# Expert weights in a ring of sixteen slots, one transfer per matrix

## The chip, the core and the metric

The kernel runs on one core of one Trainium2 chip. The time is device microseconds (us) of one execution. Beside it stands one execution taken by the hardware profiler, whose instructions and DMA packets the rows below come from. Engine names: PE is TensorE, DVE VectorE, ACT ScalarE, POOL GpSimd, SP SyncE. Everything is in 32-bit floats.

## The reference

One batch of 256 tokens, width 1024, goes through a first block (adaptive norm, gated linear attention, block attention, a dense feed-forward network) and a second one (dilated attention, a convolution, then a mixture of experts). Two thirds of the time is the last line of this:

```python
aff = softmax(h @ w_router)                      # 256 x 16
gate, idx = lax.top_k(aff.swapaxes(1, 2), 32)    # each of 16 experts takes 32 tokens
def expert(xt, w1e, w3e, w2e):                   # w1, w3: 1024 x 2816; w2: 2816 x 1024
    return (silu(xt @ w1e) * (xt @ w3e)) @ w2e
x = x + scatter_add(expert(h[idx_e], ...) * gate_e   for e in range(16))
```

Each expert has three matrices of 11.5 MB, read once: 34.6 MB an expert, 554 MB in all, for only 32 tokens each.

## The kernel before

The first 600 us hold everything up to the router. SP streams the dense matrices in "units" of three slots through an SBUF tile `ring`; PE works on them with intermediate results in a second tile, `arena`.

Then the expert phase. A slot is 2816 words a partition, 11 KB, and one matrix is 8 slots, so that an expert is 24 chunks, q = 0 to 23: w1 is 0 to 7, w3 is 8 to 15, w2 is 16 to 23. `ring` has 12 slots, and chunk q of every expert lies in slot q mod 12 (24 is a multiple of 12). SP is the only one that issues weight transfers, all on one queue (L363 to L407). It cuts an expert into eight pieces, `PIECES = (4, 4, 4, 4, 4, 2, 1, 1)` chunks (L40), each with its own semaphore `piece_in[i]`. Before each it waits on `w_used`, which PE raises by one with the last matmul of each chunk: the piece may start when the chunks that lay in its slots have been used.

PE's program for an expert is `expert(e)` (L1749). `gather` picks the 32 tokens by 16 matmuls of 32 columns with a one-hot matrix; ACT copies them to `xe` (L734). Then come the 64 matmuls of w1 (four tiles of 32 columns side by side, 352 wide), two transposes (L1791), and the 64 of w3. ACT and DVE form silu(a)*b and transpose it (L738, L1197, L1201, L1205) to `hTe`; the 88 matmuls of w2 follow; ACT copies the result out (L743); 8 matmuls scatter it with the gate weights, and DVE adds it to the output rows (L1208). Waits on `piece_in` stand at the first chunk of each piece. Expert 0 is written out, experts 1 to 15 are a loop of 15 turns (L1824).

Expert 0 is special, since its weights come while the earlier part still runs. Chunks 0 to 11 go to the ring early. Chunks 12 to 15, the last four of w3, go to `stash`, four slots' worth at the start of `arena` (L249), which are free by then. So the ring's slots 0 to 3 can take the first four chunks of expert 1 (in pieces of 1, 1 and 2, at `w_used` 1, 2 and 4) before w2 of expert 0 starts at `w_used` 8. After expert 0 the stash is not used again. `pick`, `aff` and the other live tiles of the phase lie in `arena` behind it.

A 32-bit matmul is four PE instructions (two weight loads, two passes), so the traces count two MATMUL for each one in the program. The compiled PE program has 7,843 instructions, and the body of its loop 994.

Of the kernel before, what the change touches and what calls it, by code (L numbers as in the profile page):

```python
# [15 lines left out]
C = D // P  # L16
# [16 lines left out]
FR = FE // P  # L33
DG = D // 4

SLOT = FE
NSLOT = 12
BLOCK = 3 * SLOT
NCHUNK = 24
PIECES = (4, 4, 4, 4, 4, 2, 1, 1)  # L40
AR = 14536


# [13 lines left out]
                  ("conv_ln_g_2", 4), ("conv_ln_b_2", 4), ("q_norm_g_2", 1), ("k_norm_g_2", 1)):  # L57
    VEC[_name] = (sum(n for _, n in VEC.values()), _n)
NVEC = sum(n for _, n in VEC.values())

PIECE_AT = [(sum(PIECES[:i]), n) for i, n in enumerate(PIECES)]
PIECE_OF = {q: i for i, (q, n) in enumerate(PIECE_AT)}
assert sum(PIECES) == NCHUNK and all(q % C + n <= C and q % NSLOT + n <= NSLOT for q, n in PIECE_AT)


def bank_plan():
# [53 lines left out]
def build(nc, T, out, rel_dram):  # L120
    PLAN = bank_plan()
    with ExitStack() as ctx:
        def sb(name, cols):
            return ctx.enter_context(nc.sbuf_tensor(name, [P, cols], F32))

        def sem(name):
            return ctx.enter_context(nc.semaphore(name))

        ring = sb("ring", NSLOT * SLOT)
        arena = sb("arena", AR)  # L130
        xT_ = sb("xT", C * S)
        hT_ = sb("hT", C * S)
        ident = sb("ident", P)
# [21 lines left out]
        def ex(off, words, **dims):  # L155
# [90 lines left out]
        csq = ar(0, 1024, m=CT)  # L246
        halfgb = small[:, 88:96]

        stash = ar(0, 4 * SLOT)  # L249
        yacc = xT_[:, :].rearrange("p (st n) -> p st n", st=ST)  # L250
        hnat = hT_[:, :].rearrange("p (st n) -> p st n", st=ST)
        pick = ar(11264, 1024, st=ST)
# [17 lines left out]
        emptied = [sem(f"bank_emptied{b}") for b in range(8)]  # L270
        unit_in = [sem(f"unit_in{b}") for b in range(3)]
        unit_in2 = sem("unit_in_gate_columns")
        piece_in = [sem(f"piece_in{i}") for i in range(len(PIECES))]
        s = {name: sem(name) for name in """
            x_in table_in ident_in rest_in mv_in shift_set gbias_set grs_set xg_set pv_set unit_used w_used const_set e_set attz_set attd_set
            att_set hid_used consts2_in upz_set conv_set cm_set acc_set gg2_set u2_set den_set epsd_set r1_set xr_set rsq_set qc_set cmean_set crec_set
# [1 line left out]
            sq0_set n0_set rtbneg_set relW_in t0_set hT_set ggT_set gqk_set z_set zl_set gv_set  # L278
            gr_set sgr_set b_set mqk_set klnat_set mv_set o_set osq_set gla_n max_set exp_set pT_set xmid_set
            sq1_set n1_set t1_set h_set relu_set x1_set sq2_set n3_set n2_set up_set sgb_set pe_link  # L280
            qsq_set qk_set rs16_set v_set    csq_set diag_set cvar_set x2_set sq3_set first_in stash_in lead_in sqp_set
            lge_set wr2_set std_set rst_set lgs_set hnat_set yinit_set xe_set ye_set xe_full sc_full pgT_set hid_full he_set sg_set
            ye_full out_done dve_link adacol_set adarow_set amix_set gla_set S_set mixg_set p_set
            mixm_set h2_set rs16i_set qn_set rt_set qf_set mixa_set aff_set rank_set
# [41 lines left out]
        @block.sync  # L326
        def _(sp):
            def rows(ap, c0, n):
                return ap[:, c0:c0 + n].rearrange("(c p) n -> p c n", p=P)

            def unit_source(name):
                if name.startswith("ada"):
                    return rows(T["w_ada"], D * int(name[3]), D)
                if name.startswith("win_"):
                    c0, n = {"a": (0, 2 * QKW), "v": (512, 512), "r": (1024, 512), "c": (1552, 1024)}[name[4]]
                    return rows(T["w_in"], c0, n)
                if name == "wout":
                    return rows(T["w_out"], 0, D)
                if name.startswith("ff1"):
                    return rows(T["w_ff1"], D * int(name[4]), D)  # L340
                if name.startswith("ff2"):
                    u = int(name[4])
                    return rows(T["w_ff2"][u * D:(u + 1) * D, :], 0, D)
                if name in ("conv", "qk", "v"):
                    c0, n = {"conv": (3 * MW, 2 * CW), "qk": (0, 2 * MW), "v": (2 * MW, MW)}[name]
                    return rows(T["w_in_2"], c0, n)
                return rows(T["w_out_2"], 0, D)


            for i, name in enumerate(UNITS):  # L350
                if i >= 3:
                    sp.wait_ge(s["unit_used"], FREED.index(UNITS[i - 3]) + 1)
                src = unit_source(name)
                n = src.shape[2]
                unit = unit_ap(name, C, 1024 if name == "win_v" else n)
                sp.dma_start(unit[:, :, 0:n], src).then_inc(unit_in[i % 3], 16)
                if name == "win_a":
                    o = (1 + i % 3) * BLOCK + C * 512
                    sp.dma_start(ring[:, o:o + C * RANK].rearrange("p (c n) -> p c n", c=C),
                                 rows(T["w_in"], 1536, RANK)).then_inc(unit_in2, 16)  # L360
                if name == "win_v":
                    sp.dma_start(unit[:, :, n:], rows(T["w_in"], 2576, 512)).then_inc(s["mv_in"], 16)

            mats = [T["w1_2"].rearrange("e (p c) f -> p e (c f)", p=P), T["w3_2"].rearrange("e (p c) f -> p e (c f)", p=P),
                    T["w2_2"].rearrange("e (p r) n -> p e (r n)", r=FR)]

            def slots(e, q, n, done):
                at, mat = q % NSLOT, q // C
                sp.dma_start(ring[:, at * SLOT:(at + n) * SLOT],  # L369
                             mats[mat][:, e, (q - C * mat) * SLOT:(q - C * mat + n) * SLOT]).then_inc(done, 16)  # L370

            def piece(e, i):
                slots(e, *PIECE_AT[i], piece_in[i])

            sp.wait_ge(s["unit_used"], UNIT["qk"] + 1)
            slots(0, 9, 3, s["first_in"])
            sp.wait_ge(s["unit_used"], UNIT["v"] + 1)
            sp.wait_ge(s["qf_set"], 4)
            sp.wait_ge(s["conv_set"], TAPS * CT)
            sp.wait_ge(s["xr_set"], 1)  # L380
            piece(0, 0)
            slots(0, 4, 2, s["first_in"])
            sp.wait_ge(s["unit_used"], UNIT["wo2"] + 1)
            slots(0, 6, 2, piece_in[1])
            slots(0, 8, 1, piece_in[2])
            stashed = mats[1][:, 0, (12 - C) * SLOT:]
            sp.dma_start(stash[:, 0:3 * SLOT], stashed[:, 0:3 * SLOT]).then_inc(s["stash_in"], 16)
            sp.wait_ge(s["std_set"], 1)
            sp.dma_start(stash[:, 3 * SLOT:], stashed[:, 3 * SLOT:]).then_inc(piece_in[3], 16)
            for q, n, done in ((0, 1, s["lead_in"]), (1, 1, s["lead_in"]), (2, 2, piece_in[0])):  # L390
                sp.wait_ge(s["w_used"], q + n)
                slots(1, q, n, done)
            for i, (q, n) in enumerate(PIECE_AT):
                if q > 12:
                    sp.wait_ge(s["w_used"], q + n - NSLOT)
                    piece(0, i)
            for i, (q, n) in enumerate(PIECE_AT):
                if q > 0:
                    sp.wait_ge(s["w_used"], NCHUNK + q + n - NSLOT)
                    piece(1, i)  # L400
            with sp.Fori(0, NE - 2) as e:
                for i, (q, n) in enumerate(PIECE_AT):
                    sp.wait_ge(s["w_used"], NCHUNK * e + q + n + 2 * NCHUNK - NSLOT)
                    piece(e + 2, i)


        @block.gpsimd  # L407
# [806 lines left out]
        def _(pe):  # L1214
# [531 lines left out]

            pe.sem_inc(s["pgT_full"], 1)
            pe.sem_inc(s["sc_full"], 1)
            def expert(e, first=False):  # L1749
                def gather(g):  # L1750
                    for c in range(4 * g, 4 * g + 4):
                        for st in range(ST):
# [9 lines left out]
                for mat, bank in enumerate((0, 2)):  # L1762
                    for c in range(C):
                        q = mat * C + c
                        slot = q % NSLOT
                        if mat == 0:
                            pe.wait_ge(s["xe_set"], C * e + c + 2)
                        if q in PIECE_OF:
                            pe.wait_ge(piece_in[PIECE_OF[q]], 16 * (e + 1))
                        w = ring[:, slot * SLOT:(slot + 1) * SLOT]  # L1770
                        if first and q >= 12:
                            w = stash[:, (q - 12) * SLOT:(q - 11) * SLOT]
                            pe.wait_ge(s["stash_in"], 16)
                        elif first and q >= 4:
                            pe.wait_ge(s["first_in"], 32)
                        elif q == 0 and not first:
                            pe.wait_ge(s["lead_in"], 32)
                        for half in range(2):
                            for j in range(4):
                                c0 = j * FG + half * FH  # L1780
                                ins = mm(ps[32 * j:32 * j + CAP, bank + half, 0:FH], xe[:, c, :], w[:, c0:c0 + FH],
                                         c == 0, c == C - 1)
                        ins.then_inc(s["w_used"], 1)
# [8 lines left out]
                        ins.then_inc(s["pgT_full"], 1)  # L1792
                pe.wait_ge(s["hTe_set"], e + 1)
                pe.wait_ge(s["pgT_set"], e + 1)
                w2v = ring[:, 4 * SLOT:12 * SLOT].rearrange("p (r n) -> p r n", r=FR)
                got = 0
                for r in range(FR):
                    while got * SLOT < (r + 1) * D:
                        q = 2 * C + got
                        if q in PIECE_OF:  # L1800
                            pe.wait_ge(piece_in[PIECE_OF[q]], 16 * (e + 1))
                        got += 1
                    for j in range(4):
                        ins = mm(ps[32 * j:32 * j + CAP, 4, 0:DG], hTe[:, r, :], w2v[:, r, j * DG:(j + 1) * DG],
# [15 lines left out]
                                 ye[32 * j:32 * j + CAP, :], True, True)  # L1820
                    ins.then_inc(s["sc_full"], 1)

            expert(0, first=True)
            with pe.Fori(1, NE) as e:  # L1824
                expert(e)


def S_at(Sst, n, mt):
# [83 lines left out]
```

## Time and profile before

| | us |
|---|---|
| median of 3 runs | 1854.61 |
| lowest, highest | 1854.27, 1855.59 |
| the profiled execution's own time | 1853.62 |
| its span, first to last instruction | 1851.9 |

Around the span 1.72 us of the profiled execution are outside the instructions. It lies 0.99 us under the median. In the span, PE has records for 73% of the time, PE's weight loads for 45%, DVE 15%, ACT 12%, POOL 2%. 649 MB are moved.

### The profile page before, as it was taken

The page shows a single profiled execution, that of the slowest core. Times are in us where ns is not written, and L with a number is a line of the kernel's source. Part 1 is how long each engine was busy: PE and PEld are TensorE (multiplying, and loading weights), DVE is VectorE, ACT ScalarE, POOL GpSimd, SP SyncE. Part 2 cuts the span into 40 slices and gives each one's busy share as a digit, 9 for nine tenths or more (in the row PEclk, how much of TensorE's full clock was granted, in tenths as well). Part 3 has the DMA queues.
Part 4 walks back from the last instruction along what each step waited for, and adds up shares of the span by engine and source line. Part 5 has one row for each costly group of instructions (what it writes and reads, how often), then busy time and mean ns, then how long its engine had stood idle before and what let it go on. Part 6 is the DMA issues. An engine that isn't in the chain of part 4 may idle for free.

```text
span 1851.9 us, 24026 instructions
## 1 busy us (share of the span) xinstructions
PE 1353.7 (73%) x10574; PEld 831.9 (45%) x10574; DVE 274.7 (15%) x559; ACT 226.6 (12%) x530; POOL 39.4 (2%) x64
## 2 busy tenths in 40 slices
PE   6998999999987777476666757566655665756665
PEld 4576888888655334142332414234232322413232
DVE  1215100006952001000010100001000000100001
ACT  1333222012133010000100001010000100000010
POOL 0000000002020000000000000000000000000000
PEclk9999999999998777777777777877777787777778
DMA  9746363341444899999999999999999999999998
GB/s 351 299 163 242 114 250 145 128 182 68 185 187 187 372 436 435 427 430 433 438 428 429 435 429 435 430 435 435 427 431 428 442 422 436 435 431 426 430 441 342
DMA packets 48248, 649.02 MB, mean 350 GB/s; under 512 B 3832, under 2 KB 6336, under 8 KB 31056
## 3 DMA queue, kind: packets, MB, share of 16 engines
q1 hardware_dynamic: 45152, 643.90, 82.4%
q10 hardware_dynamic: 2848, 3.55, 0.6%
q0 software_dynamic: 208, 1.00, 0.1%
q8 instruction: 30, 0.49, 0.1%
q14 instruction: 10, 0.08, 0.0%
HBM read 647.38 MB, written 1.06 MB: 350 GB/s over the span
## 4 chain that ended last, share of the span: by engine, by line
DMA 59%; PE 11%; DVE 1%; ACT 1%; issue 0%; SPq 0%; PEldq 0%; DVEq 0%; ACTq 0%
DMA ring<-in_w 59%; PE ps L1216 11%; DVE arena L1113 0%; ACT arena L678 0%; ACT arena L525 0%; DVE arena L1164 0%; DVE arena L1166 0%; DVE xT L1208 0%; ACT L701 0%; ACT L678 0%; ACT arena L688 0%; ACT arena L687 0%; DVE arena L1183 0%; SPq L369 0%; DVE arena L1079 0%
## 5 line engine op out<-in xcount | busy, mean ns | idle before, releaser
L1216 PE MATMUL ps<-ring,table 128*32 128x352 f32 x4032 | 435.3, 602 | 269.4 <-DMA ring<-in_w 269.3
L1216 PEld LDWEIGHTS ps<-ring,table 128*32 128x32 f32 x4032 | 154.1, 140 | 535.5 <-issue 340.4
L1216 PE MATMUL ps<-ring,arena 128*32 128x256 f32 (+1 forms) x2818 | 197.3, 438 | 148.9 <-DMA ring<-in_w 148.6
L1216 PEld LDWEIGHTS ps<-ring,arena 128*32 128x32 f32 (+1 forms) x2818 | 103.2, 125 | 245.1 <-issue 149.0
L1216 PE MATMUL ps<-hT,ring 128*128 128x256 f32 (+1 forms) x880 | 194.6, 382 | 3.0 <-PE ps L1216 1.4
L1216 PEld LDWEIGHTS ps<-hT,ring 128*128 128x128 f32 (+1 forms) x880 | 165.0, 189 | 30.8 <-issue 5.9
L1216 PE MATMUL ps<-arena,ring 128*128 128x256 f32 (+1 forms) x800 | 175.1, 379 | 1.9 <-ACT arena L627 1.4
L1216 PEld LDWEIGHTS ps<-arena,ring 128*128 128x128 f32 x800 | 151.5, 190 | 23.3 <-issue 2.9
L1216 PE MATMUL ps<-arena 32*128 32x256 f32 (+10 forms) x532 | 96.4, 396 | 31.7 <-DVE xT L1208 12.2
L1216 PEld LDWEIGHTS ps<-arena,hT 128*128 128x128 f32 x512 | 106.3, 320 | 9.4 <-issue 9.4
L1216 PE MATMUL ps<-arena,hT 128*128 (+1 forms) x512 | 108.4, 392 | 1.8 <-DVEq L1192 1.8
L743 ACT ACTIVATE arena<-ps 128x256 f32<-128x256 f32 x16 | 6.2, 384 | 731.0 <-PEq L1809 731.0
L1208 DVE TENSOR_TENSOR xT<-xT,ps 128x512 f32<-128x512 f32 x64 | 41.8, 685 | 343.7 <-PE ps L1216 343.7
L1216 PEld LDWEIGHTS ps<-arena 32*128 32x128 f32 (+7 forms) x532 | 62.5, 189 | 64.6 <-issue 34.5
L1197 DVE TENSOR_TENSOR arena<-arena,ps 128x704 f32<-128x704 f32 x16 | 14.2, 888 | 429.7 <-ACT arena L738 429.7
L1201 DVE TENSOR_TENSOR arena<-arena,ps 128x704 f32<-128x704 f32 x16 | 14.2, 888 | 376.3 <-PEq L1785 376.3
L1014 DVE SCALAR_TENSOR_TENSOR arena<-arena,table 128x256 f32<-128x256 f32 x120 | 52.9, 508 | 1.2 <-DVE arena L1048 0.2
L738 ACT ACTIVATE arena<-ps 128x704 f32<-128x704 f32 x16 | 12.1, 758 | 285.6 <-PEq L1785 285.6
L1216 PE MATMUL ps<-ring,hT 128*128 128x512 f32 x96 | 44.5, 615 | 0.5 <-ACT hT L520 0.4
L734 ACT ACTIVATE table<-ps,table 128x32 f32<-128x32 f32 x128 | 26.3, 288 | 140.2 <-PE ps L1216 140.2
L1216 PE MATMUL ps<-ring 128*128 128x256 f32 (+5 forms) x200 | 41.0, 388 | 2.2 <-PE ps L1216 1.4
L466 POOL TENSOR_TENSOR arena<-arena 128x128 f32 x32 | 12.1, 399 | 1168.1 <-PE ps L1791 1105.2
(223 smaller groups left out, 542.8 us busy)
## 6 DMA issues: line engine op xcount, KB each, us to landing
ring<-in_w SPq DMA_DIRECT2D x76, 5632.0 KB, 32.9
ring<-in_w SPq DMA_DIRECT2D x19, 2816.0 KB, 28.4
ring<-in_w SPq DMA_DIRECT2D x35, 1408.0 KB, 31.3
ring<-in_w_ff SPq DMA_DIRECT2D x8, 4096.0 KB, 14.0
ring<-in_w_ada SPq DMA_DIRECT2D x6, 4096.0 KB, 13.8
ring<-in_w_in SPq DMA_DIRECT2D x3, 4096.0 KB, 14.4
ring<-in_w_in SPq DMA_DIRECT2D x5, 2048.0 KB, 19.2
ring<-in_w_out SPq DMA_DIRECT2D x2, 4096.0 KB, 12.8
```

The costliest lines, as they stand in the source:

```text
L466: ins = nc.gpsimd.tensor_tensor(pgs[:, st, :].rearrange("p (j t) -> p j t", j=4), pick[:, st, bass.ds(e * CAP, CAP)].unsqueeze(1).broadcas ...
L734: A(xe[:, c, :], ps[:, (7, 3)[c // 4], c * CAP:(c + 1) * CAP], ACT.Copy, scale=g2rows[:, c:c + 1])\
L738: A(sge.rearrange("p (a b) -> p a b", a=2), ps[:, 0:2, 0:FH], ACT.Sigmoid).then_inc(s["sg_set"], 1)
L743: A(ye, ps[:, 4, 0:DG], ACT.Copy).then_inc(s["ye_set"], 1)
L1014: ins = V.scalar_tensor_tensor(dst, src, w, dst, ALU.mult, ALU.add)
L1197: V.tensor_tensor(he.rearrange("p (a b) -> p a b", a=2), sge.rearrange("p (a b) -> p a b", a=2), ps[:, 0:2, 0:FH], ALU.mult).then_inc(s["h ...
L1201: V.tensor_tensor(he.rearrange("p (a b) -> p a b", a=2), he.rearrange("p (a b) -> p a b", a=2), ps[:, 2:4, 0:FH], ALU.mult).then_inc(s["he ...
L1208: V.tensor_tensor(yacc[:, :, j * DG:(j + 1) * DG], yacc[:, :, j * DG:(j + 1) * DG], ps[:, 5 + j % 2, :].rearrange("p (st n) -> p st n", st ...
L1216: return pe.matmul(o, w, x, start=first, stop=last)
```

## The change

The tiles `ring` and `arena` become one tile `big`, laid out in the same order and the same size. `ring` is now its first 16 slots, the last four of which are what was the stash; `arena` still starts behind slot 12. The ring is used as two halves of eight slots. A matrix of an expert fills one half, and the next matrix the other. As an expert has three matrices, an expert with an odd number starts in the other half (`odd`).

For experts 1 to 14 each matrix is one transfer of eight slots: 90,112 bytes a partition, 11.5 MB, issued when the matrix two before it has been used up. Each has one semaphore, `third_in[0..2]`. w2 of expert 0 comes in 1, 1, 2, 4 chunks, w2 of the last expert in 4, 2, 1, 1. The early transfers of expert 0 keep their order and sizes. PE waits once before each matrix instead of at each piece. Its loop body now holds two experts, an odd and an even one, in 7 turns, and expert 15 is written out behind it. The compiled PE program has 9,800 instructions, and its loop body 1,983.

```diff
-NSLOT = 12
+UNIT_SLOTS = 12
+NSLOT = 16
-PIECES = (4, 4, 4, 4, 4, 2, 1, 1)
+FIRST_W2 = (1, 1, 2, 4)
+LAST_W2 = (4, 2, 1, 1)
...
-        ring = sb("ring", NSLOT * SLOT)
-        arena = sb("arena", AR)
+        big = sb("big", UNIT_SLOTS * SLOT + AR)
+        ring = big[:, 0:NSLOT * SLOT]
+        arena = big[:, UNIT_SLOTS * SLOT:]
...
-            def slots(e, q, n, done):
-                at, mat = q % NSLOT, q // C
+            def slots(e, q, n, done, odd=0):
+                at, mat = (q + 8 * odd) % NSLOT, q // C
...
-            for q, n, done in ((0, 1, s["lead_in"]), (1, 1, s["lead_in"]), (2, 2, piece_in[0])):
-                sp.wait_ge(s["w_used"], q + n)
-                slots(1, q, n, done)
...
+            q = 2 * C
+            for i, n in enumerate(FIRST_W2):
+                sp.wait_ge(s["w_used"], q + n - NSLOT)
+                slots(0, q, n, w2_in[i])
+                q += n
+            def thirds(e, odd, count=3):
+                for mat in range(count):
+                    sp.wait_ge(s["w_used"], NCHUNK * e + C * (mat + 1) - NSLOT)
+                    slots(e, C * mat, C, third_in[mat], odd)
+            with sp.Fori(1, NE - 1, 2) as e:
+                thirds(e, 1)
+                thirds(e + 1, 0)
+            thirds(NE - 1, 1, 2)
...
-            expert(0, first=True)
-            with pe.Fori(1, NE) as e:
-                expert(e)
+            expert(0, 0, first=True)
+            with pe.Fori(1, NE - 1, 2) as e:
+                expert(e, 1)
+                expert(e + 1, 0)
+            expert(NE - 1, 1, last=True)
```

SP's program in its loop over the experts, one turn, before (`in_w_2` stands for the three expert tensors; 11264 words are four slots, 5632 two and 2816 one):

```order
L369 DMA ring<-in_w_2 128x11264 [waits w_used]
L403 REGISTER_ALU
L369 DMA ring<-in_w_2 128x11264 [waits w_used]
L403 REGISTER_ALU
L369 DMA ring<-in_w_2 128x11264 [waits w_used]
L403 REGISTER_ALU
L369 DMA ring<-in_w_2 128x5632 [waits w_used]
```

And the same engine after, half a turn of its loop, which is one expert:

```order
L368 ISA [waits w_used]
L368 DMA big<-in_w_2 128x2x11264
L368 DMA big<-in_w_2 128x2x11264 [waits w_used]
L393 REGISTER_ALU
L368 DMA big<-in_w_2 128x2x11264 [waits w_used]
```

Five transfers of four slots, one of two and two of one have become three of eight, and each of the three is built as two runs of 11,264 words a partition.

PE at the end of its loop before: the w2 matmuls of an expert, the scatter, and the branch that closes the turn of one expert.

```order
L1216 MATMUL ps<-ring,arena 32x256 x88
L1808 REGISTER_ALU
L1811 REGISTER_ALU
L1815 ISA
L1216 MATMUL ps<-arena 128x256 x4
L1817 REGISTER_ALU
L1216 MATMUL ps<-arena 128x256 x2
L1817 REGISTER_ALU
L1216 MATMUL ps<-arena 128x256 x2
L1824 REGISTER_ALU
L1824 COMPARE_AND_BRANCH
```

PE after, at the end of its loop and at the start of what stands behind it:

```order
L1216 MATMUL ps<-big 128x256 x2
L1820 REGISTER_ALU
L1216 MATMUL ps<-big 128x256 x2
L1827 REGISTER_ALU
L1827 COMPARE_AND_BRANCH
L1216 MATMUL ps<-big,hT 128x32 x16
L1216 MATMUL ps<-big,table 32x352 x64
L1791 MATMUL ps<-ident,big 128x128 x2
L1216 MATMUL ps<-big,table 32x352 x64
L1216 MATMUL ps<-big 32x256 x88
L1216 MATMUL ps<-big 128x256 x8
```

The matmuls of an expert are the same and in the same order; the branch comes after every second expert, and a written-out expert follows it.

## Rows read from the trace of the kernel before

**Rows 1.** The page: span, PE, granted clock and GB/s in 40 slices.
```profile
span 1851.9 us, 24026 instructions
PE 1353.7 (73%) x10574; PEld 831.9 (45%) x10574; DVE 274.7 (15%) x559; ACT 226.6 (12%) x530; POOL 39.4 (2%) x64
...
PEclk9999999999998777777777777877777787777778
...
GB/s 351 299 163 242 114 250 145 128 182 68 185 187 187 372 436 435 427 430 433 438 428 429 435 429 435 430 435 435 427 431 428 442 422 436 435 431 426 430 441 342
```

**Rows 2.** The page: chain that ended last, by engine, share of the span.
```profile
DMA 59%; PE 11%; DVE 1%; ACT 1%; issue 0%; SPq 0%; PEldq 0%; DVEq 0%; ACTq 0%
```

**Rows 3.** The chain in order of time: start us, us, what.
```profile
653.88 0.04 issue
...
720.95 0.04 issue
...
1682.37 0.04 issue
1682.41 1.55 PE ps L1216 x24
1683.97 38.38 DMA ring<-in_w
...
1762.48 0.04 issue
...
1842.57 0.04 issue
```

**Rows 4.** PE's and DVE's timeline, last expert: start, us, line, operation, idle before.
```profile
1762.53 1.50 PE L1216 MATMUL ps<-ring,arena 128*32 128x256 f32 x24 [1.88 <-DMA ring<-in_w]
...
1768.55 7.04 PE L1216 MATMUL ps<-arena,hT 128*128 x32
...
1775.86 7.74 PE L1216 MATMUL ps<-ring,table 128*32 128x352 f32 x64 [0.28 <-DMA ring<-in_w]
...
1789.27 7.86 PE L1216 MATMUL ps<-ring,table 128*32 128x352 f32 x64 [5.67 <-DMA ring<-in_w]
...
1802.51 6.37 PE L1216 MATMUL ps<-ring,table 128*32 128x352 f32 x64 [4.64 <-DMA ring<-in_w]
...
1815.84 6.53 PE L1216 MATMUL ps<-ring,table 128*32 128x352 f32 x64 [6.96 <-DMA ring<-in_w]
...
1823.46 1.79 DVE L1205 STREAM_TRANSPOSE arena<-arena 128x704 f32<-128x704 f32 x1
...
1829.26 8.97 PE L1216 MATMUL ps<-ring,arena 128*32 128x256 f32 x128 [6.88 <-DMA ring<-in_w]
...
1842.61 1.50 PE L1216 MATMUL ps<-ring,arena 128*32 128x256 f32 x24 [1.86 <-DMA ring<-in_w]
```

**Rows 5.** The page: weight transfers issued, KB each, median us to landing.
```profile
ring<-in_w SPq DMA_DIRECT2D x76, 5632.0 KB, 32.9
ring<-in_w SPq DMA_DIRECT2D x19, 2816.0 KB, 28.4
ring<-in_w SPq DMA_DIRECT2D x35, 1408.0 KB, 31.3
```

**Rows 6.** PE's timeline, all eight slots of expert 0's and 1's w1.
```profile
607.34 11.36 PE L1216 MATMUL ps<-ring,table 128*32 128x352 f32 x128
...
667.46 12.01 PE L1216 MATMUL ps<-ring,table 128*32 128x352 f32 x128
```

**Rows 7.** Window from 610 us: busy us by engine, PEclk, DMA share, GB/s.
```profile
610.00:615.00 5.00, 5.00 (x68) 1.90 (x64) 0.00 (x0) 0.00 (x0) 0.00 (x0) 0.92 0.82 291
```

**Rows 8.** DMA queues, 0 to 600 us: packets, MB, share of 16 engines.
```profile
q8 instruction: 23, 0.38, 0.2%
```

**Rows 9.** The same from 654 to 722 us, the loop's first turn.
```profile
q1 hardware_dynamic: 1015, 29.15, 99.8%
q8 instruction: 4, 0.07, 0.4%
```

**Rows 10.** The same from 722 to 1846 us, the loop's other turns.
```profile
DMA packets 16093, 482.84 MB, mean 430 GB/s; under 512 B 1792, under 2 KB 1792, under 8 KB 1792
...
q1 hardware_dynamic: 16092, 482.83, 99.8%
q14 instruction: 1, 0.01, 0.0%
```

More of the change, by code:

```diff
@@ L59 @@
 NVEC = sum(n for _, n in VEC.values())
-PIECE_AT = [(sum(PIECES[:i]), n) for i, n in enumerate(PIECES)]
-PIECE_OF = {q: i for i, (q, n) in enumerate(PIECE_AT)}
-assert sum(PIECES) == NCHUNK and all(q % C + n <= C and q % NSLOT + n <= NSLOT for q, n in PIECE_AT)
 def bank_plan():
@@ L247, in build @@
         halfgb = small[:, 88:96]
-        stash = ar(0, 4 * SLOT)
         yacc = xT_[:, :].rearrange("p (st n) -> p st n", st=ST)
@@ L272, in build @@
         unit_in2 = sem("unit_in_gate_columns")
-        piece_in = [sem(f"piece_in{i}") for i in range(len(PIECES))]
+        third_in = [sem(f"third_in{i}") for i in range(3)]
+        w2_in = [sem(f"w2_in{i}") for i in range(4)]
         s = {name: sem(name) for name in """
@@ L280, in build @@
             sq1_set n1_set t1_set h_set relu_set x1_set sq2_set n3_set n2_set up_set sgb_set pe_link
-            qsq_set qk_set rs16_set v_set    csq_set diag_set cvar_set x2_set sq3_set first_in stash_in lead_in sqp_set
+            qsq_set qk_set rs16_set v_set    csq_set diag_set cvar_set x2_set sq3_set first_in stash_in lead_in mid_in edge_in sqp_set
             lge_set wr2_set std_set rst_set lgs_set hnat_set yinit_set xe_set ye_set xe_full sc_full pgT_set hid_full he_set sg_set
@@ L365, in _ @@
                     T["w2_2"].rearrange("e (p r) n -> p e (r n)", r=FR)]
-            def slots(e, q, n, done):
-                at, mat = q % NSLOT, q // C
+            def slots(e, q, n, done, odd=0):
+                at, mat = (q + 8 * odd) % NSLOT, q // C
                 sp.dma_start(ring[:, at * SLOT:(at + n) * SLOT],
                              mats[mat][:, e, (q - C * mat) * SLOT:(q - C * mat + n) * SLOT]).then_inc(done, 16)
-            def piece(e, i):
-                slots(e, *PIECE_AT[i], piece_in[i])
             sp.wait_ge(s["unit_used"], UNIT["qk"] + 1)
@@ L380, in _ @@
             sp.wait_ge(s["xr_set"], 1)
-            piece(0, 0)
+            slots(0, 0, 4, s["lead_in"])
             slots(0, 4, 2, s["first_in"])
             sp.wait_ge(s["unit_used"], UNIT["wo2"] + 1)
[L384 to L387, printed above, removed]
+            slots(0, 6, 2, s["mid_in"])
+            slots(0, 8, 1, s["mid_in"])
+            slots(0, 12, 3, s["stash_in"])
             sp.wait_ge(s["std_set"], 1)
-            sp.dma_start(stash[:, 3 * SLOT:], stashed[:, 3 * SLOT:]).then_inc(piece_in[3], 16)
-            for q, n, done in ((0, 1, s["lead_in"]), (1, 1, s["lead_in"]), (2, 2, piece_in[0])):
-                sp.wait_ge(s["w_used"], q + n)
-                slots(1, q, n, done)
[L393 to L404, printed above, removed]
+            slots(0, 15, 1, s["edge_in"])
+            q = 2 * C
[11 more added lines that the diff above has]
+            thirds(NE - 1, 1, 2)
+            q = 2 * C
+            for i, n in enumerate(LAST_W2):
+                sp.wait_ge(s["w_used"], NCHUNK * (NE - 1) + q + n - NSLOT)
+                slots(NE - 1, q, n, w2_in[i], 1)
+                q += n
         @block.gpsimd
@@ L1748, in _, with expert @@
             pe.sem_inc(s["sc_full"], 1)
-            def expert(e, first=False):
+            FIRST_AT = ((0, s["lead_in"], 1), (4, s["first_in"], 2), (6, s["mid_in"], 2),
+                        (12, s["stash_in"], 1), (15, s["edge_in"], 1))
+            def expert(e, odd, first=False, last=False):
                 def gather(g):
@@ L1764, in expert @@
                         q = mat * C + c
-                        slot = q % NSLOT
+                        slot = (q + 8 * odd) % NSLOT
                         if mat == 0:
                             pe.wait_ge(s["xe_set"], C * e + c + 2)
-                        if q in PIECE_OF:
-                            pe.wait_ge(piece_in[PIECE_OF[q]], 16 * (e + 1))
-                        w = ring[:, slot * SLOT:(slot + 1) * SLOT]
[L1771 to L1777, printed above, removed]
+                        if first:
+                            for at, done, n in FIRST_AT:
+                                if q == at:
+                                    pe.wait_ge(done, 16 * n)
+                        elif c == 0:
+                            pe.wait_ge(third_in[mat], 16 * e)
+                        w = ring[:, slot * SLOT:(slot + 1) * SLOT]
                         for half in range(2):
@@ L1794, in expert @@
                 pe.wait_ge(s["pgT_set"], e + 1)
-                w2v = ring[:, 4 * SLOT:12 * SLOT].rearrange("p (r n) -> p r n", r=FR)
+                w2v = ring[:, 8 * odd * SLOT:8 * (odd + 1) * SLOT].rearrange("p (r n) -> p r n", r=FR)
+                steps = FIRST_W2 if first else LAST_W2 if last else (C,)
+                starts = [sum(steps[:i]) for i in range(len(steps))]
                 got = 0
@@ L1798, in expert @@
                     while got * SLOT < (r + 1) * D:
-                        q = 2 * C + got
-                        if q in PIECE_OF:
-                            pe.wait_ge(piece_in[PIECE_OF[q]], 16 * (e + 1))
+                        if got in starts and (first or last):
+                            pe.wait_ge(w2_in[starts.index(got)], 16 * (1 + odd))
+                        elif got == 0:
+                            pe.wait_ge(third_in[2], 16 * e)
                         got += 1
```

## The prediction

> **What bounds the kernel now.** I read the page first: from slice 14 on, some 650 us, the GB/s row stands at 422 to 442 without a hole, while PE's clock is granted at seven to eight tenths, a mean over its two levels of 1.2 and 2.4 GHz, which means that PE stops and starts [rows 1]. The chain of waits gives the DMA queue 59% of the span and PE 11% [rows 2]. In order of time the chain repeats: a stretch of PE, then 30 to 38 us of weight transfer [rows 3]. The same point of two successive experts is 1762.48 and 1842.57, 80.09 us apart, and so is 1682.37 from 1762.48, 80.11 us. An expert is 34.6 MB, so this is 432 GB/s. Does PE or SP hold the queue back anywhere? A four-slot transfer lands 32.9 us after its issue [rows 5], and one such transfer moves in 13.33 us: PE, which waits for each, starts at 1789.27, 1802.51, 1815.84 and 1829.26, 39.99 us for three [rows 4]. So about one and a half transfers always stand queued ahead of it. The expert phase is a pipe at its rate. PE idles 4.6 to 7 us before each of these pieces [rows 4]. The time can only move by what each byte costs in the pipe, by holes in it, by other traffic in it, or by what lies before its first and behind its last byte.
>
> **What the change takes off the pipe.** The number of bytes is the same. Six times 13.33 is 79.98 us, while an expert takes 80.10; as five four-slot pieces take 66.65, the four slots that come as 2, 1, 1 take 13.45. The two extra pieces cost 0.12 us, 0.06 each. Fifteen such groups go (w2 of experts 1 to 14, and the 1, 1, 2 of expert 1; the small ones of expert 0's and expert 15's w2 stay): 15 x 0.12 = 1.8 us, say 2.0 with the completion writes saved. That holds if the cost belongs to each row of each partition, because a row of 90 KB is still built as two runs of 45 KB, the size of a four-slot row. If it belongs to each transfer, thirds go on to save three more an expert, 3 x 0.06 x 15 = 2.9, together 4.9 us. I take 2.0: the change's own program shows the two runs. In a sentence by itself: the Trainium skill, page "DMA: Bandwidth & Descriptors", section "Anatomy of one DMA", fits a fixed 2.0 us a DMA, and five fewer in each of 15 experts would be 150 us if it were exposed; the trace has 0.06 us for a piece, since the next is queued already, so that part of the rule is hidden here.
>
> **Does the pipe get holes?** A third may be issued when the third two before it has been used up. At that moment the third between is in flight, 26.67 us long. PE needs for eight slots after a pause 11.36 and 12.01 us [rows 6]; for w2, 8.97 + 1.5 + 1.5 = 12.0 us [rows 4]. So the next issue comes with 26.67 - 12 = 14.7 us still to move. What an issue needs until it flows is small: the first weight issue of the phase is at 609.98, and the window 610 to 615 is already 82% busy, under 1 us lost [rows 7]. Even a PE that took 7.86 us for every four slots, the slowest half in the rows, leaves 11 us. Before w1 there is more in the way: behind w2's last landing come 1.5 us of matmuls, and w1's first matmul starts 11.8 us after those end (copy, scatter, add, gather, `xe`) [rows 4]. With w2 whole: 12.0 + 11.8 = 23.8 us, against 26.67 until w1 lands. Free by 2.9 us, and if it were late only this slack of 14.7 us would shrink. No hole; price 0.
>
> **The start.** SP's first wait in the phase is `w_used` 1 as before, then 2, 4, 8 with the same sizes 1, 1, 2, 4; only the source is w2 of expert 0 and not w1 of expert 1. w1 of expert 1 is issued at `w_used` 16, when PE is through two matrices, some 22 us after the first slot was used; until then 8 slots or 26.7 us are queued. 0.
>
> **The end.** The last w2 still comes as 4, 2, 1, 1. But w3 now comes whole, at 1815.84 in the old time, and PE has eight slots to do from there, not four. 12.0 instead of 6.53 us, then the 2.9 us that the old trace has from the end of those matmuls (1822.37) to the end of DVE's transpose (1825.25) [rows 4]: w2 can start at 1830.75, not 1829.26. Its first 128 instructions 8.97, the next 24 1.5: 1841.2. The last slot lands at 1842.57. Covered by 1.3 us. If the cover is gone (15.7 us for w3, twice the slowest half burst): 3.7 us later, 2.4 us on the end.
>
> **What the change adds to the pipe.** The page has a queue of its own for instructions. PE's code comes through it in packets of 16.4 KB (0.38 MB in 23) [rows 8]. The program of before has 7,843 instructions and 30 packets came, one for 256. They come for straight code throughout, 23 before 600 us. In the loop's first turn 4 come [rows 9], and in the 14 turns after it none on that queue [rows 10]: the store keeps a body of 994 instructions, which touches five blocks. The new body has 1,983, which with its start in the middle of a block touches nine, ten with one ahead. The rows show that five blocks stay, and that the store is small enough to be refilled at each boundary from the first 100 us on. Whether ten stay they don't show. If a body is larger than the store and blocks are dropped in turn, every block of it misses in every turn: 6 more turns x 9 to 10 = 57 fetches. I hold that for the likelier, as the body doubles and the kept five would be doubled too. By itself: the Trainium skill, page "Runtime: NRT & Kernel Launch", section "Instruction fetch mechanics", gives PE 128 KiB in blocks of 16 KiB, so eight; nine would not fit, and each taken branch out of the store would stall. The same section also speaks of two lines only; the loop of before, kept in five, speaks against that.
>
> What does a fetch cost? 0.4% of 16 engines x 68 us / 4 = 1.1 us of one DMA engine [rows 9]; the 16 engines each carry a share of every transfer, and a landing waits for the slowest. In the first turn four fetches moved the landings little: 653.88 to 720.95 is 67.07 us for 20 slots, against 80.09 - 13.33 = 66.76 later, 0.31 us or 0.08 a fetch [rows 3]. They fell on different engines, then. But the queue never runs dry, so an engine never catches up, and a second hit on the same one counts whole. 57 + 8 new one-time fetches (9,800 instructions against 7,843) + the 7 old ones in the phase are 72 on 16 engines: 4.5 each, the most hit 5, against 1 before. Four rounds x 1.2 us (1.1 and a little for the weight packet beside it, my choice; no row prices that) = 4.8 us. From below: a fetch costs only its bytes, 16.4 KB of 432 GB/s, 0.04 us, x 65 = 2.5 us. From above: the ten blocks have each a fixed engine, hit in each of 6 turns: 6 x 1.2 = 7.2 us. PE itself waits for the block at the branch back, some 3 us I'd guess from 1.1 us plus a weight packet ahead, once in 160 us, just at the gather, where 2.9 us are free and then 14.7: 0.
>
> **Sum,** against the profiled execution: 1851.9 - 2.0 + 4.8 = 1854.7 of span; with the 1.72 us around it 1856.4; the median was 0.99 above, 1857.4 us.
>
> **The rivals.**
> Kept: the store holds the body. -2.0, +0.6 for 8 more one-time fetches at 0.08: 1853.2 us. For it: five blocks are kept without a trace of trouble [rows 10]. By the number of instructions alone the body, 1,983, would just fit the 2,048 of the Trainium skill's page "Runtime: NRT & Kernel Launch".
> Kept, and the cost per transfer goes: -4.9 + 0.6: 1850.3. Against it: the two runs of 45 KB.
> Fetches on fixed engines: -2.0 + 7.2: 1859.8, slower. It decides from four hits on one engine in the phase on. Nothing in the rows says how blocks are dealt out, except that the first few fell apart.
> Only bytes: -2.0 + 2.5: 1855.1. Speaks for it: 0.08 us a fetch in the first turn; against, that others' lead hid it.
> The tail uncovered, w3's burst slow: +2.4 on any case; up to 1859.8 on mine. Against: both bursts of eight slots took 12 us or less [rows 6].
>
> **How the numbers follow.** Forecast (fetched again, dealt in turn) 0.40; only bytes 0.12; kept 0.18; kept and per transfer 0.06; fixed engines 0.18; tail uncovered or a hole in the pipe 0.06. The range leaves out the per-transfer case and the worst of the fixed engines (1.4 us a hit gives 1861): 1851.5 to 1861.0. A measurement can tell about 0.2%, 3.7 us, from no change. Faster by more: the per-transfer case and a bit, 0.07. Slower by more, over 1858.3: fixed engines, the tail, and 0.12 of my forecast's 0.40 (1.4 us a hit gives 1858.2), 0.36. Within: 0.57.
>
> **What would show it.** The instruction queue q8 has 92 to 98 packets, not 30, and some in every stretch of the phase; 38 would mean that the body is kept. The time between the same points two experts apart (160.2 us before) is 159.9 if kept and about 160.7 if fetched again; 159.5 if the cost was the transfer's. Weight transfers: 11,264 KB, packets of the same 45 KB. PE's bursts of w1 and w3 are 128 instructions in 11 to 13 us. A stop of PE before the gather of every odd expert would be the block at the branch. Behind the last landing the same 9.3 us as before, from 1842.57 to the span's end. I am wrong if DMA falls under 0.97 in windows of the loop, or if w3's burst at the end runs over 13.3 us, or if an expert's time moves by over 1 us.

## The result, and the profile after

| | before | changed |
|---|---|---|
| median, us | 1855.01 (5 runs) | 1864.59 (5 runs) |
| lowest, highest | 1854.27, 1855.59 | 1863.82, 1866.08 |
| span of the profiled execution | 1851.9 | 1862.9 |

The ratio is 1.0056 with a 95% interval of 1.0044 to 1.0069: slower by 0.56%, some 10 us. The forecast was 1857.4, at most 1861.0. The likeliest case was a loss of 2.8 us, too small to be told from no change; its sign was right, its size was not, and the time lies outside the range.

The lines below are the page of the changed kernel, to be read against [rows 1, 2, 5, 8]: span, PE, granted clock, GB/s in 40 slices, the instruction queue, the chain by engine, and the weight transfers.

```profile
span 1862.9 us, 23681 instructions
...
PE 1288.1 (69%) x10574; PEld 823.2 (44%) x10574; DVE 275.0 (15%) x559; ACT 226.8 (12%) x530; POOL 39.4 (2%) x64
...
PEclk9998999999998967767776676777677676777778
...
GB/s 348 316 165 220 114 248 152 119 181 67 183 186 214 388 432 432 432 431 432 432 432 430 432 430 428 430 432 432 423 432 431 431 417 432 432 423 432 431 432 304
...
q8 instruction: 98, 1.61, 0.3%
...
DMA 51%; PE 19%; issue 1%; DVE 1%; ACT 1%; SPq 0%; PEldq 0%; DVEq 0%; ACTq 0%
...
big<-in_w SPq DMA_DIRECT2D x44, 11264.0 KB, 41.6
```

PE works on the same 10,574 records. The 44 large transfers are there. What has changed is q8: 98 instruction packets instead of 30. The GB/s row looks like a full pipe, with values that fall to 417 and 423 in a few slices. PE's granted clock is 0.795 on the mean instead of 0.833; the runs below show that the loss doesn't follow the clock (0.822 and a larger loss in the first of them).

Two experts are one turn of PE's loop. The DMA queues' view of such a stretch, from 882 to 1044 us, gives packets, MB and the share of 16 engines:

```profile
q1 hardware_dynamic: 1639, 69.57, 99.6%
q8 instruction: 10, 0.16, 0.4%
```

In the kernel before, q8 has no packet in such a stretch [rows 10]. The chain of the changed kernel in order of time, at points where w2 of an even expert has landed (the end of a turn of PE's loop), and where the last slot of all has:

```profile
801.55 0.14 issue
...
963.04 0.14 issue
...
1124.52 0.14 issue
...
1286.09 0.14 issue
...
1610.41 0.14 issue
...
1853.43 0.04 issue
```

Three turns take 161.49, 161.48 and 161.57 us. Over five turns (801.55 to 1610.41) the mean is 161.77, because the next one takes 162.89 (1286.09 to 1448.98), against 160.2 before [rows 3]. Six thirds at the undisturbed pace take 159.9 (it is measured below). So 1.9 us a turn on the mean go with ten packets of code, 0.16 MB beside the 69.57 MB on the weights' queue. The last slot lands 10.86 us later (1853.43 against 1842.57), which is all of the 11.0 us that the span grew by, but for 0.1.

### The profile page after: what moved, and what is told of

It reads as the page before. It is cut to its first block, busy times and chain, and to the rows that moved or that the text cites. A ratio compares the mean times of both kernels' runs of the same rounds, so it can differ in the third digit from the quotient of the medians.

```text
span 1862.9 us, 23681 instructions
## 1 busy us (share of the span) xinstructions
PE 1288.1 (69%) x10574; PEld 823.2 (44%) x10574; DVE 275.0 (15%) x559; ACT 226.8 (12%) x530; POOL 39.4 (2%) x64
## 4 chain that ended last, share of the span: by engine, by line
DMA 51%; PE 19%; issue 1%; DVE 1%; ACT 1%; SPq 0%; PEldq 0%; DVEq 0%; ACTq 0%
DMA big<-in_w 51%; PE ps L1216 19%; DVE big L1113 0%; ACT big L678 0%; DVE xT L1208 0%; ACT big L525 0%; DVE big L1164 0%; DVE big L1166 0%; ACT L701 0%; ACT L678 0%; ACT big L688 0%; ACT big L687 0%; DVE big L1183 0%; ACT big L743 0%; DVE big L1079 0%
## 5 line engine op out<-in xcount | busy, mean ns | idle before, releaser
L1216 PE MATMUL ps<-big 128*32 128x256 f32 (+6 forms) x4350 | 501.6, 419 | 261.8 <-DMA big<-in_w 223.2
L1216 PEld LDWEIGHTS ps<-big 128*32 128x32 f32 (+5 forms) x4350 | 351.0, 148 | 411.1 <-issue 295.9
L1216 PE MATMUL ps<-big,table 128*32 128x352 f32 x4096 | 375.3, 533 | 211.8 <-DMA big<-in_w 211.8
L1216 PEld LDWEIGHTS ps<-big,table 128*32 128x32 f32 x4096 | 138.9, 126 | 433.2 <-issue 218.6
L1216 PE MATMUL ps<-big,hT 128*128 (+2 forms) x608 | 156.8, 432 | 58.8 <-issue 56.5
L1216 PE MATMUL ps<-hT,big 128*128 128x256 f32 (+1 forms) x880 | 194.3, 382 | 3.0 <-PE ps L1216 1.5
L1216 PEld LDWEIGHTS ps<-hT,big 128*128 128x128 f32 (+1 forms) x880 | 165.6, 189 | 30.0 <-issue 4.9
L1216 PEld LDWEIGHTS ps<-big,hT 128*128 128x128 f32 x608 | 127.1, 305 | 91.9 <-issue 91.6
L1014 DVE SCALAR_TENSOR_TENSOR big<-big,table 128x256 f32<-128x256 f32 x120 | 52.9, 505 | 1.2 <-DVE big L1048 0.2
L1205 DVE STREAM_TRANSPOSE big<-big 128x704 f32<-128x704 f32 x16 | 28.6, 1789 | 0.6
L625 ACT ACTIVATE big<-ps 128x256 f32<-128x256 f32 x30 | 11.5, 383 | 82.0 <-PE ps L1216 71.2
```

The costliest lines, as they stand in the source:

```text
L625: A(h1[:, m, :], bk(f"f{m}")[:, 0:S], ACT.Relu).then_inc(s["relu_set"], 1)
L1014: ins = V.scalar_tensor_tensor(dst, src, w, dst, ALU.mult, ALU.add)
L1205: V.transpose(hTe, he.rearrange("p (q r) -> p r q", r=FR)).then_inc(s["hTe_set"], 1)
L1216: return pe.matmul(o, w, x, start=first, stop=last)
```

## Experiments

There are two theories. **F**: the loop body on PE no longer stays in its instruction store, its blocks (256 instructions, 16 KB each) are fetched again in every turn, and each fetch delays the weight pipe. **G**: the coarse grain costs (holes in the pipe, slower transfers, or a PE that is late).

One thing has to be allowed for when last landings of two kernels are compared: the stages before the weight phase end up to 1.3 us earlier or later from one profiled execution to another. The first weight issue of the phase is at 609.98 us in the kernel before, 609.49 in the changed one, and between 608.64 and 611.03 in the others. "From the first issue" below means that this start is taken off. SP's timeline, 600 to 612 us, before and after:

```profile
609.98 2.02 SPq L369 DMA_DIRECT2D ring<-in_w  x2
...
609.49 1.60 SPq L368 DMA_DIRECT2D big<-in_w  x2
```

### Two experts a turn on the old ring

```diff
-            with pe.Fori(1, NE) as e:
-                expert(e)
+            with pe.Fori(1, NE - 1, 2) as e:
+                expert(e)
+                expert(e + 1)
+            expert(NE - 1)
```

> The kernel before, with its ring of 12 and its eight pieces, but with PE's loop over the experts written with two experts a turn (7 turns) and the last one written out. Only TensorE's code grows, to a loop body of 1,987 instructions. If the code fetched again is what costs (theory F): some 98 instruction packets on q8, ten in each of the six later turns, and by the after trace's 1.7 us for ten fetches 6 x 1.7 = 10.2 us, with the one-time fetches 1.4 more: 1866 us. If the coarse transfers cost (theory G: an 8-slot grain that leaves holes in the weight pipe or makes PE late): as before, 1855 us, within 1 us.

It took 1867.28 us against 1853.70, ratio 1.0074 (1.0057 to 1.0091). Below are the queue of instructions from its page, and the last landing in its chain:

```profile
q8 instruction: 98, 1.61, 0.3%
...
1855.68 0.04 issue
```

98 packets, exactly as in the changed kernel, with transfers that are the old ones. The old ring with the new loop is even slower than the changed kernel, 13.1 us on the last landing, 14.1 from the first issue. So the loss needs no large transfer at all: the loop brings it, as F says. Whether it is the fetches or the stop at the branch is not told apart here. The changed kernel is the better of the two by what its larger pieces save.

### The large transfers with a short body

```diff
-                        for half in range(2):
+                        for half in range(2 if mat == 0 else 1):
...
-                    for j in range(4):
+                    kept = r in (0, FR - 1) or any((k * SLOT - 1) // D == r for k in range(1, C + 1))
+                    for j in range(4 if kept else 0):
```

> The changed kernel with all its transfers and waits, but with a shorter loop body on TensorE, 1,311 instructions: half of the w3 matmuls and about two thirds of the w2 matmuls are left out (the result is not the reference's). Theory F: the body stays in the store, some 33 instruction packets, and what is left is the saving of the larger pieces: 1852.5 us (1851 to 1854). Theory G with holes in the pipe from the grain: no change in the transfers and their order, 1862 to 1865 us.

It took 1855.66 us against 1853.70, ratio 1.0006 (0.9997 to 1.0016). That is not the loss of 10 us, but not the gain of 1 to 2 either. Here are its instruction queue and the end of its chain:

```profile
q8 instruction: 33, 0.54, 0.1%
...
1842.14 0.04 issue
1842.19 1.98 PE ps L1216 x16
...
1844.71 2.08 PE ps L1216 x8
...
1847.56 2.68 PE ps L1216 x8
```

Each transfer ends with 16 packets of 4 bytes, the completion writes, as many as there are DMA engines. The last of them is 26.65 to 26.67 us behind that of the matrix before, for matrix after matrix from 721 to 1787 us: 79.96 us an expert. With whole matrices and no fetches the pipe has no holes, and G falls, as far as it is about the transfers; that PE is not late with all of its work stands under the written-out kernel. Why then no gain? The last slot lands 0.43 us earlier than before, 1.0 from the first issue, not 2.3. One code block is fetched while w3 of the last expert comes, and that third takes 27.67 us, 1.0 more; another, early, costs 0.5. That leaves 0.8 of the 2.3, near the 1.0. And this PE has so little to do that its scatter at the end ran slower, 2.08 and 2.68 us where the last scatter of before shows 1.14 and 1.7. Its granted clock from 1844 to 1854 us is 0.50, the level of 1.2 GHz, against 0.86 in the kernel before from 1844 to 1852: the end is 11.7 us behind the last landing and not 9.3. That 2.4 us belongs to the left-out work, not to the transfers.

### How large is the store, and does the dose count?

This is the kernel before, one expert a turn, with idle matmuls of 16 columns that lengthen the body. They stand ahead of each matrix in the loop (and the same ahead of w2):

```diff
+PAD_MM = 58
...
+                        for k in range(PAD_MM if c == 0 and not first else 0):
+                            mm(ps[32 * (k % 4):32 * (k % 4) + CAP, bank, 0:16], xe[:, c, :], w[:, 0:16], True, True)
```

> The kernel before, one expert a turn, with 174 idle matmuls of 16 columns a turn (58 ahead of each matrix, results overwritten by the real ones), which make the loop body 1,691 instructions: it touches eight blocks of 256. TensorE has idle time for them. Theory F with a store of eight blocks that also fetches one ahead: nine are wanted, all are fetched again in 14 turns, 9 x 14 = 126 fetches more, at 0.17 us each 21 us: 1876 us. If the store is larger than nine blocks: 1855 us. Theory G: 1855 us, unless the matmuls themselves are late.

The middle one has 38 in place of 58:

> As the longer one, but with 114 idle matmuls a turn: a loop body of 1,451 instructions that touches seven blocks. Theory F with a store of eight blocks: seven and one ahead fit, 32 instruction packets, 1855.3 us. If the store were smaller (six or seven blocks), 8 x 14 = 112 fetches, 1874 us. If the idle matmuls themselves cost by making PE late, this one shows it without fetches.

The third is the long one with 30 such matmuls once, ahead of the loop:

```diff
+            for k in range(30):
+                mm(ps[32 * (k % 4):32 * (k % 4) + CAP, 4, 0:16], hTe[:, 0, :], hTe[:, 0, 0:16], True, True)
             with pe.Fori(1, NE) as e:
```

> The long padded kernel (body 1,691 instructions, 159 fetches, 1880 us) with 30 more idle matmuls ahead of the loop, once. The body is the same in length, but now starts 0.2 blocks behind a boundary and not 0.7, and touches seven blocks of 256 instead of eight. Theory F with a store of eight blocks, one of them fetched ahead: all is kept, 33 packets, 1855 us. If what counts is the body's length, or if idle matmuls cost by themselves: 1880 us as before.

The long one took 1880.36 us (two runs) against 1853.70, ratio 1.0144 (1.0124 to 1.0164). The middle one took 1854.89, ratio 1.0007 (0.9996 to 1.0017). The long one, shifted, took 1856.40 against 1854.14, ratio 1.0014 (1.0004 to 1.0025). The instruction queue in the pages of the three, in this order:

```profile
q8 instruction: 159, 2.61, 0.6%
```
```profile
q8 instruction: 32, 0.52, 0.1%
```
```profile
q8 instruction: 33, 0.54, 0.1%
```

The first and the last have the same loop body, 1,691 instructions in the compiled programs; only where it starts differs. At 0.73 of a block it touches eight blocks and is 24 us slower; at 0.2 it touches seven and stays. This pair is the strongest evidence in the case: the same loop, transfers and branch, and only the fetches differ, with the stops that PE makes for them. The body of 1,451 also touches seven. So whole blocks count, not instructions. The numbers come out to the packet: 33 + 14 turns x 9 (eight and one ahead) = 159, and 38 + 6 x 10 (nine and one ahead) = 98. A store of eight blocks of which one runs ahead explains the count of every kernel here; the store itself is inferred from the counts. Once one block is missing, all of them are fetched in each turn. The idle matmuls themselves cost at most the 1.2 and 2.3 us of the kernels that stay, and two or three more one-time fetches account for most of that (see "Where the fetches fall").

### All experts written out, large transfers

```diff
-            with pe.Fori(1, NE - 1, 2) as e:
-                expert(e, 1)
-                expert(e + 1, 0)
+            for e in range(1, NE - 1):
+                expert(e, e % 2)
```

> The changed kernel with its whole-matrix transfers, but with all 16 experts written out on TensorE: 21,422 instructions, no loop, no branch back. Each block is fetched once, 83 packets in all, some 61 of them in the expert phase, against 75 of the changed kernel. Theory F, in which each fetch in the full pipe costs what it costs whether it is the first or a repeated one (0.175 us each in the after trace): 14 x 0.175 = 2.5 us below the changed kernel, 1862 us, and TensorE shows no stop of 4 to 7 us ahead of the gather. If it is not the fetches but the stop at the branch back that costs: 1853 to 1855 us.

It took 1861.23 us against 1854.14, ratio 1.0037 (1.0023 to 1.0051), with 83 packets, as counted. A fetch costs the same whether it is the first or a repeated one. What this kernel doesn't have is the stop at the branch back. In the changed kernel the view of waits, 722 to 1846 us (total, times, longest), and PE's timeline at one such place show that stop:

```profile
PE ps L1216 <- issue: 56.5, 12, 6.8
```
```profile
1625.69 2.35 PE L1216 MATMUL ps<-big 32*128 32x256 f32 x8 [0.76 <-DVE xT L1208]
1632.83 2.33 PE L1216 MATMUL ps<-big,hT 128*128 x10 [4.78 <-issue]
1638.99 4.91 PE L1216 MATMUL ps<-big,hT 128*128 x22 [3.83 <-issue]
1643.83 11.27 PE L1216 MATMUL ps<-big,table 128*32 128x352 f32 x128
...
1664.99 10.94 PE L1216 MATMUL ps<-big,table 128*32 128x352 f32 x128 [9.05 <-DMA big<-in_w]
```

There are twelve stops, two for each of six branches back, ahead of the gather and inside it: 4.78 and 3.83 us here. w1 is used up only at 1655.1, yet w3 lands at 1664.9, so the next issue still came with 9.8 us left to move. The closest of the six turns is this one, where the next issue went out at 848.69 us and w3 landed at 854.9:

```profile
825.76 2.34 PE L1216 MATMUL ps<-big,hT 128*128 x10 [6.58 <-issue]
831.59 4.90 PE L1216 MATMUL ps<-big,hT 128*128 x22 [3.49 <-issue]
836.42 12.20 PE L1216 MATMUL ps<-big,table 128*32 128x352 f32 x128
...
854.93 5.27 PE L1216 MATMUL ps<-big,table 128*32 128x352 f32 x44 [5.47 <-DMA big<-in_w]
```

The last completion write of that w3 came at 854.41, so 5.7 us were left. The stops are real and free: PE with all of its work is not late either. The 3 us between this kernel and the changed one are what 15 fetches fewer give, at 0.20 each 3.0.

### Even pieces on the old ring

```diff
+EVEN = (4, 4, 4, 4, 4, 4)
...
-            with sp.Fori(0, NE - 2) as e:
-                for i, (q, n) in enumerate(PIECE_AT):
-                    sp.wait_ge(s["w_used"], NCHUNK * e + q + n + 2 * NCHUNK - NSLOT)
-                    piece(e + 2, i)
+            with sp.Fori(0, NE - 3) as e:
+                for i in range(6):
+                    sp.wait_ge(s["w_used"], NCHUNK * e + 4 * i + 4 + 2 * NCHUNK - NSLOT)
+                    slots(e + 2, 4 * i, 4, piece_in[i])
+            for i, (q, n) in enumerate(PIECE_AT):
+                sp.wait_ge(s["w_used"], NCHUNK * (NE - 1) + q + n - NSLOT)
+                piece(NE - 1, i)
...
-            with pe.Fori(1, NE) as e:
+            with pe.Fori(1, NE - 1) as e:
                 expert(e)
+            expert(NE - 1, last=True)
```

> The kernel before with one expert a turn and its ring of 12, but with w2 of experts 1 to 14 in two pieces of four slots instead of 4, 2, 1, 1; the last expert is written out, with 4, 2, 1, 1. Does the saving of larger pieces exist at all? 14 x 0.13 to 0.16 us = 1.8 to 2.2 us off the pipe, against four more one-time fetches (0.2 to 1.0 us in all): 1 us under the kernel before, 1852.7 us; an expert in 79.96 instead of 80.11 us in its trace. If the size of pieces is nothing, 80.11 and 1854 us.

It took 1852.46 us against 1854.14, ratio 0.9991 (0.9982 to 1.0001): the sum came out, but the runs can't tell it from no change. The trace can. Here is its chain at the same point of successive experts, and at the last landing:

```profile
1601.49 0.04 issue
...
1681.45 0.04 issue
...
1761.41 0.04 issue
...
1842.86 0.04 issue
```

An expert takes 79.96 us, where before it was 80.11 and 80.09 [rows 3]. That is 0.15 us for two pieces fewer, and the thirds gave no more than that (79.96 too, with three pieces fewer again): the cost is that of a row, not of a transfer. Then the last expert takes 81.45 us instead of 80.1. It is the one written out, and its four blocks of code cost 1.3 us, a good half of the 2.1 saved. That this last landing stands at 1842.86, 0.29 us later than before, is the start: from the first issue (611.03 against 609.98) it is 0.76 earlier, as 2.1 less 1.3 asks for.

## Where the fetches fall

The packet records don't name their engine, but the 16 completion writes of a transfer do show how far the engines are apart, taking it that each engine writes one. Computed from the packet records, for one transfer a row: the time of its first completion write in us, then how much later each of the 16 came, sorted.

```
before       1826.5  0.0 0.1 0.1 0.2 0.3 0.3 0.4 0.4   1.2 1.7 1.8 1.8 1.8 2.0 2.1 2.2
written out   930.0  0.0 0.0 0.1 0.1 0.3 0.3 0.5 0.9   3.2 3.2 3.3 3.3 3.5 3.5 3.5 3.9
written out  1276.4  0.0 0.0 0.1 0.1 0.3 0.3 0.6 0.9   6.4 6.4 6.4 6.5 6.6 6.6 6.7 7.0
written out  1809.4  0.0 0.0 0.1 0.2 0.3 0.3 0.6 1.0   11.1 11.1 11.1 11.2 11.3 11.6 12.9 13.0
changed      1144.1  0.0 0.0 0.2 0.2 0.2 0.2 0.3 0.4   6.2 6.4 6.5 6.5 6.5 6.6 6.7 7.4
```

Eight engines stay together through the whole phase. The other eight fall behind, and evenly: in the written-out kernel none gets much further before all eight have come up to the same step. So the fetches go in turn, but over eight of the 16 engines. In the kernel before, the seven fetches of the phase have reached nearly each of the eight once, and that is all.

What one hit costs follows from the same writes: from 664 to 1171 us in the changed kernel the lags of all engines grow by 48.8 us in sum, with 31 fetches, and from 664 to 1809 in the written-out one by 85.3 us with 54: 1.57 and 1.58 us each. The packet records agree: a code packet takes 1.07 us on the mean in the written-out kernel (722 to 1810 us), and as many weight packets as there are code packets, 52, take 2.13 to 2.22 us instead of 1.67. An engine that fell behind never catches up, since it always has weights queued, and each landing waits for the last engine. So a round of eight fetches costs one hit, 1.6 us, and one fetch an eighth of it, 0.20 us. Its 16 KB alone are 0.04 us of the pipe. It also explains the uneven turns: ten fetches are one round and a quarter, so most turns hold one step of the landings and some hold two (162.89 us). That a turn shows 1.9 us fits ten fetches at 0.20. What chooses the eight engines stays open.

The eight engines without code run up to 9.7 us ahead in the changed kernel, and then they do run dry: in the turn in which PE's two stops add up to the most, 10.4 us, the first completion write of a transfer comes 30.10 us behind that of the one before and not 26.65 (1492.14 to 1522.24). That costs nothing, as the last writes of the same two transfers are 26.73 us apart.

The price can be checked on the last landings from the first issue, 1232.59 us in the kernel before, with the 2.25 us (15 x 0.15) that the larger pieces save added back where the transfers are large:

| kernel | first issue | last landing | longer than before | with the saving | fetches more | each |
|---|---|---|---|---|---|---|
| changed | 609.49 | 1853.43 | 11.35 | 13.60 | 68 | 0.20 |
| two experts a turn, old ring | 609.02 | 1855.68 | 14.07 | 14.07 | 68 | 0.21 |
| written out | 608.64 | 1849.82 | 8.59 | 10.84 | 53 | 0.20 |
| long padded | 610.77 | 1869.52 | 26.16 | 26.16 | 129 | 0.20 |

Counted in rounds it fits the small cases too. The middle padded kernel has nine fetches in the phase instead of seven, so it begins a second round, and its last landing is one hit later, 1.6 us (1843.27 with the first issue at 609.04); the shifted one has ten and is 1.4 later (1844.78, 610.79).

The long padded kernel's last landing in its chain:

```profile
1869.52 0.04 issue
```

## Why the prediction was wrong

**What bounds the kernel.** Right. The pipe bounds both kernels; the loss is all in the time between the first and the last byte.

**What the change takes off.** The forecast was 2.0 us; 15 x 0.15 = 2.3 were measured through the even pieces. Right, and by the row of each partition rather than by the transfer, as taken. The 4.9 us bound is excluded. The fixed 2.0 us of the Trainium skill that the prediction sets beside this is that section's fit for DMAs issued on GpSimd's path; those here are issued by SP, and no run here shows such a cost.

**Holes.** None that a landing waits for: right, and so were the numbers, as bursts of eight slots take 10.9 to 12.6 us in the changed kernel. The guess of a 3 us stop at the branch was too small. It is 8.6 us in two parts in the turn shown and 10.4 at the most, more than the 2.9 free before w1; the larger cover behind it, 14.7 us, held with 9.8 left, 5.7 at the least.

**The end.** Right. From the changed kernel's PE timeline, last expert:

```profile
1825.27 11.01 PE L1216 MATMUL ps<-big,table 128*32 128x352 f32 x128 [13.53 <-DMA big<-in_w]
...
1839.86 4.96 PE L1216 MATMUL ps<-big 128*32 128x256 f32 x88 [3.58 <-DMA big<-in_w]
```

w3's burst took 11.0 us, w2 still waited for its weights, and the end is 9.5 us behind the last landing, 9.3 before.

**What the change adds.** The step that failed is the price of the fetches, 4.8 us. That the body would be dropped was right, and so was the number: 98 packets, at the upper end of what was forecast. The rule cited from the Trainium skill, page "Runtime: NRT & Kernel Launch", section "Instruction fetch mechanics", a store of eight blocks of 16 KiB for this engine, agrees with the 7 blocks that stay and the 8 that don't; its remark on two lines does not hold here. That the fetches are dealt in turn was right too. But I took them as dealt over 16 engines, 72 fetches or four rounds more than before, of 1.2 us each. They go in turn over eight: 75 fetches in the phase against seven, 8.5 rounds more, of 1.57 us each, 13.4 us. The number of engines is the larger of the two errors, a factor of two; the cost of a hit is the smaller: the slower weight packet beside the code, 0.5 us, was put at 0.1. The rival with fixed engines was nearer in size, 7.2 us, but only half of the measured, and its way of dealing is not what the writes show.

In the rows there was a sign that I read too far: 0.08 us a fetch in the first turn shows that those four fell on different engines, and that fits eight engines as well as 16, with seven fetches in the whole phase. The number of engines was a term of the sum for which no row stood, and eight or fewer would have needed a place among the rivals.

With this price, worked out from the completion writes and not from the loss, the sum closes: -2.3 + 13.4 = +11.1 us, against +11.35 on the last landing from the first issue, and +11.0 on the span.

## What to carry to other kernels

In a kernel that a full DMA queue bounds, code is traffic too: count the instructions of a loop body, and in which blocks of 256 it lies, before unrolling it once more. Here one body of 1,691 instructions cost 24 us or nothing, depending on where it began. A delay on one DMA engine is paid in full when that engine's queue never runs dry, so price small extra packets by the engine that gets most of them and not by their bytes; the lags of a transfer's completion writes show which share of the engines that is. And a piece that is larger than needed saves only its rows' overhead, 0.15 us in 80 here.

## What the hardware showed that I had not expected

- The instruction queue's packets fell in turn on eight of the 16 DMA engines and left the other eight alone (lags of 11.1 to 13.0 us against 0.0 to 1.0 in the written-out kernel), with 1.6 us lost on an engine for a packet of 16 KB.
- When a loop body is one block too large for the store, every block is fetched in every turn (9 of 9, 10 of 10), not only the one that doesn't fit.
- A branch back to a dropped block stops TensorE twice, 4.8 and 3.8 us in the turn shown, in a pipe that is full of weight packets.
